# Sample steps of a hybrid decoder: cached rows turned on VectorE, scores in 32x32 tiles, copies on ScalarE

## What is computed

```python
def mla_sample(q_nope, q_rope, ckv_new, kr_new, cache_lat, cache_kr, page_table, w_uk, w_uv):
    lat_past = cache_lat[page_table].reshape(Bd, -1, MLA_KV_RANK)      # 8 x 4096 x 128
    kr_past = cache_kr[page_table].reshape(Bd, -1, MLA_ROPE)           # 8 x 4096 x 32
    q_lat = jnp.einsum('bshn,rhn->bshr', q_nope, w_uk)
    s_past = jnp.einsum('bshr,btr->bhst', q_lat, lat_past) + jnp.einsum('bshp,btp->bhst', q_rope, kr_past)
    ...
    p = jax.nn.softmax(s, axis=-1).astype(lat_all.dtype)
    o_lat = jnp.einsum('bhst,btr->bshr', p, lat_all)
    return jnp.einsum('bshr,rhv->bshv', o_lat, w_uv)
```

## Time and profile before

| | us |
|---|---|
| median of 3 runs (745.23 to 751.47) | 745.68 |
| profiled execution, device time | 743.97 |
| its span, first to last instruction | 742.1 |
| mean granted TensorE clock | 0.995 of full speed |
| TensorE busy | 705.5 (95%) |
| VectorE busy | 355.3 (48%) |
| ScalarE busy | 327.3 (44%) |
| GpSimd busy | 75.6 (10%) |
| HBM read, written | 62.26 MB, 6.07 MB |

### The profile page before, as it was taken

One profiled execution on the slowest core, in us unless ns is written; L12 is line 12 of the kernel. 1 busy time (PEld: TensorE's weight loads), 2 busy tenths in 40 slices (PEclk: granted clock), 3 DMA queues, 4 the chain that ended last, 5 costly groups with the idle time before them and its releaser, 6 DMA issues.

```text
span 742.1 us, 16684 instructions
## 1 busy us (share of the span) xinstructions
PE 705.5 (95%) x7025; PEld 546.4 (74%) x7025; DVE 355.3 (48%) x782; ACT 327.3 (44%) x779; POOL 75.6 (10%) x113
## 2 busy tenths in 40 slices
PE   2799999999999999999999999999999999999995
PEld 1486878788789986777766666777677889678884
DVE  0454380030202025777675576667671111389977
ACT  1254651121212137667656566645675667602100
POOL 0000000000000010101111201132113443000000
PEclk9999999999999999999999999999999999999999
DMA  9995300303001011000010000202756774103332
GB/s 293 396 375 174 114 0 1 114 0 97 0 1 57 1 43 51 9 14 11 10 11 1 1 1 1 59 1 76 240 183 222 274 267 175 60 1 116 123 132 85
DMA packets 35301, 70.31 MB, mean 95 GB/s; under 512 B 6626, under 2 KB 17979, under 8 KB 33564
## 3 DMA queue, kind: packets, MB, share of 16 engines
q1 hardware_dynamic: 30602, 47.73, 19.8%
q0 software_dynamic: 4016, 20.97, 8.1%
q10 hardware_dynamic: 610, 0.55, 0.3%
HBM read 62.26 MB, written 6.07 MB: 92 GB/s over the span
## 4 chain that ended last, share of the span: by engine, by line
PE 90%; DVE 3%; SPq 2%; DMA 2%; ACT 1%; issue 1%; another core or an unknown queue 1%; DVEq 0%; ACTq 0%
PE banks L1988 21%; PE banks L2174 8%; PE banks L2000 6%; PE banks L2302 5%; PE banks L2383 4%; PE banks L2403 3%; PE banks L2152 3%; PE banks L2512 3%; PE banks L2514 3%; PE banks L2513 2%; PE banks L2090 2%; PE banks L2009 2%; PE banks L2452 2%; PE banks L2471 2%; PE banks L2495 2%; DMA s_x<-in_x_prompt 2%
## 5 line engine op out<-in xcount | busy, mean ns | idle before, releaser
L1044 ACT ACTIVATE s_z<-banks 128x512 f32<-128x512 f32 (+3 forms) x40 | 19.6, 501 | 130.0 <-PE banks L1988 130.0
L1988 PE MATMUL banks<-s_w_parts,s_h_b 128*128 128x272 f32 (+3 forms) x328 | 68.0, 323 | 0.0
L1253 ACT ACTIVATE s_z<-banks 128x512 f32<-128x512 f32 (+2 forms) x88 | 41.4, 517 | 47.1 <-PE banks L2383 46.3
L1417 DVE COPY s_zs<-banks 8x512 f32<-8x512 f32 (+3 forms) x6 | 3.5, 576 | 118.5 <-PE banks L1962 118.5
L1988 PEld LDWEIGHTS banks<-s_w_parts,s_h_b 128*128 128x128 f32 x328 | 49.3, 189 | 4.9 <-issue 1.7
L1244 ACT ACTIVATE s_z<-banks,s_temps 128x896 f32<-128x896 f32 (+7 forms) x64 | 47.2, 742 | 11.6 <-DVE s_temps L1712 8.6
L1988 PE MATMUL banks<-s_w_parts,s_h_a 128*128 128x256 f32 (+2 forms) x256 | 49.7, 314 | 0.0
L1988 PE MATMUL banks<-s_z_r,s_h_b 128*128 128x512 f32 (+1 forms) x152 | 48.8, 387 | 0.0
L2383 PEld LDWEIGHTS banks<-s_ident,s_z 128*128 128x128 f32 x288 | 33.3, 141 | 11.8 <-issue 5.5
L2383 PE MATMUL banks<-s_ident,s_z 128*128 128x128 f32 x288 | 39.8, 274 | 1.6 <-DVE s_z L1728 1.6
L1988 PE MATMUL banks<-s_z_r,s_h_a 128*128 128x512 f32 x128 | 40.9, 395 | 0.0
(11 more groups left out here) (391 smaller groups left out, 1520.7 us busy)
## 6 DMA issues: line engine op xcount, KB each, us to landing
s_z<-in_w_ada SPq DMA_DIRECT2D x16, 512.0 KB, 12.2
s_temps<-in_w_in SPq DMA_DIRECT2D x3, 2048.0 KB, 7.7
s_x<-in_x_prompt SPq DMA_DIRECT2D x8, 512.0 KB, 11.8
s_z<-in_w_ada SPq DMA_DIRECT2D x1, 4096.0 KB, 13.8
s_kt<-in_w_out SPq DMA_DIRECT2D x8, 512.0 KB
s_temps<-in_x_prompt SPq DMA_DIRECT2D x8, 512.0 KB
out_y_prompt<-s_temps SPq DMA_DIRECT2D x7, 512.0 KB
s_temps<-in_w_in SPq DMA_DIRECT2D x2, 832.0 KB, 14.2
```

Of the source, the lines that this page charges most:

```text
L1253: nc.scalar.activation(PTb[r % 3][:, 4 * g:4 * g + n, :], banks[:, 4 + (groups(r) + g) % 2, 0:P * n].rearrange("p (j q) -> p j q", j=n), A ...
L1988: last = nc.tensor.matmul(banks[:, proj_bank(c, t), 0:WIDTH[c]], h_[half][:, k, n0:n0 + P], w_, start=(k == 0 and n == 0), stop=(k == KT - ...
```

## The change

Nothing outside the sample steps is computed differently. In words:

- TensorE no longer transposes cached rows. VectorE turns them in SBUF with its own transpose, which turns each 32x32 block in place: two instructions of 128x1024 (`keys_turned`) and one of 128x512 (`rotary_turned`) for each step. Those of step n + 1 come before and after the maximum of step n. Unit 0 is turned at the end of the prompt's score steps.
- Because only blocks are turned, the contraction is split into four groups of 32 partitions that hold different tokens, and into k = 0 to 3 for the four quarters of the 128 numbers, and k = 4 for the rotary part. The scores are 5 x 4 x 4 = 80 matmuls of 32x32 weights with 128 columns; row group g writes to bank g, column group c to partitions 32c on. The result is 128 partitions by 4 x 128 columns; on each 32 partitions only the first eight, the heads, mean something.
- The queries are stored as 32x32 pieces (`q_tiles`), filled by 16 small copies on VectorE from `q_lat`.
- The maximum goes over 512 columns in four banks and the exponential over 512 columns; the weights are turned by four transposes instead of one.
- The copies of turned weights and of weighted sums move from VectorE to ScalarE; ScalarE's five copies of turned rows are gone.
- `p_s` has one buffer instead of two, and the scores four banks with one buffer.
- The gate products move from the end to steps 3, 5, 7 and 9, into banks 4 and 5; the copies of w_out are placed differently among ScalarE's last steps.
- In the merge, one more VectorE instruction (`nm_own`) masks the meaningless partitions.

The diff, cut to its core:

```diff
-        qlw = carve(NB * 56, NB, 56)
-        qrw = carve(NB * 32, NB, 32)
+        q_lat = carve(NB * H)
+        q_tiles = carve(NB * 5 * H + 24)
+        nm_own = carve(NB * SPLITS, NB, SPLITS)
         o_new = carve(NB * (KVR + 1), NB, KVR + 1, rows=H)
...
+        def latT(n, half):
+
+            return slab(FIRST_KEYS[half]) if n % 2 == 0 else latT1[:, SEQ * half:SEQ * half + SEQ]
+
...
+        def tile_queries(b, k):
+
+            c0 = H * (5 * b + k)
...
+        GATES_AT = (3, 5, 7, 9)
...
+            def weights(n):
+
+                act.wait_ge(f_mx, n + 1)
+                if n >= 1:
+                    act.wait_ge(f_pT, n)
+                b, c = divmod(n, HALVES)
+                nc.scalar.activation(p_s.rearrange("p (r g y) -> p g r y", r=4, g=4), banks[:, 0:4, 0:P].rearrange("p g (r y) -> p g r y", r=4),
+                                     ACT.Exp, bias=nm[:, b, c:c + 1], accum_out=o_all[:, b, c, KVR:KVR + 1]).then_inc(f_p, 1)
...
+            def weights_out(n):
+                act.wait_ge(f_pT, n + 1)
                 if n >= 2:
-                    act.wait_ge(f_sc, n - 1)
...
+                    act.wait_ge(f_o, n - 1)
+                nc.scalar.activation(pTx[n % 2].rearrange("p (g r) q -> p r g q", g=4)[:, :, :, 0:H],
+                                     banks[:, 6, :].rearrange("p (r g q) -> p r g q", r=4, g=4)[:, :, :, 0:H], ACT.Copy).then_inc(f_pTc, 1)
...
+            def values_out(n):
...
+                act.wait_ge(f_o, n + 1)
+                nc.scalar.activation(o_all[:, b, c, 0:KVR], banks[:, 7, 0:KVR], ACT.Copy).then_inc(f_oc, 1)
...
-            keys_out(0, 4)
             act.wait_ge(mixed, N_PAIRS_OF_HEADS)
-            for j in range(5):
-                keys_out(1, j)
-            weights(0)
+            act.wait_ge(p_padded, 7)
             for n in range(NSTEPS):
-                if n + 2 < NSTEPS:
-                    for j in range(5):
-                        keys_out(n + 2, j)
-                if n + 1 < NSTEPS:
-                    weights(n + 1)
-                if n == NSTEPS - 4:
+                weights(n)
+                if n > 0:
+                    values_out(n - 1)
+                weights_out(n)
+                for q in range(2):
+                    if n == GATES_AT[q] + 1:
+                        act.wait_ge(gate_b, q + 1)
+                        nc.scalar.activation(gateP[:, 512 * q:512 * q + 512], banks[:, 4 + q, :], ACT.Copy).then_inc(gate_bc, 1)
+                    if n == GATES_AT[2 + q] + 1:
+                        act.wait_ge(gate_b, q + 3)
+                        nc.scalar.activation(gateS[:, 512 * q:512 * q + 512], banks[0:NB, 4 + q, :], ACT.Copy).then_inc(gate_bc, 1)
...
                     high_mixed(0)
...
                     act.wait_ge(f_o, 13)
-                    act.wait_ge(f_sc, 15)
-                    for k in range(4):
+                    for k in range(2):
                         high_out(k)
                 if n == NSTEPS - 2:
+                    act.wait_ge(f_sc, 15)
+                    for k in range(2, 4):
+                        high_out(k)
+                if n == NSTEPS - 1:
                     act.wait_ge(f_o, 14)
                     high_out(4)
                     high_out(5)
                     act.wait_ge(f_o, 15)
                     high_out(6)
+                    values_out(n)
                     high_out(7)
...
-            act.wait_ge(gate_b, 2)
-            for q in range(2):
-                nc.scalar.activation(gateP[:, 512 * q:512 * q + 512], banks[:, q, :], ACT.Copy).then_inc(gate_bc, 1)
-                nc.scalar.activation(gateS[:, 512 * q:512 * q + 512], banks[0:NB, 2 + q, :], ACT.Copy).then_inc(gate_bc, 1)
...
+                    nc.vector.tensor_copy(q_tiles[:, 0:NB * 5 * H].rearrange("p (b k h) -> p b k h", b=NB, k=5)[:, :, 4, :],
+                                          banks[:, 7, 64:128].rearrange("p (h b) -> p b h", h=H)).then_inc(p_free, 1)
                 if n == PREP["qlat"]:
                     dve.wait_ge(p_pe, n)
-                    nc.vector.tensor_copy(qlw[:, :, 24:24 + H], banks[:, 7, 0:64].rearrange("p (h b) -> p b h", h=H)).then_inc(p_free, 1)
+                    nc.vector.tensor_copy(q_lat.rearrange("p (b h) -> p b h", b=NB),
+                                          banks[:, 7, 0:64].rearrange("p (h b) -> p b h", h=H)).then_inc(p_free, 1)
...
+                if PREP["qlat"] <= n < PREP["qlat"] + 4:
+                    k = n - PREP["qlat"]
+                    dve.wait_ge(p_free, PREP["qlat"])
+                    for g in range(4):
+                        nc.vector.tensor_copy(q_tiles[32 * g:32 * g + 32, 0:NB * 5 * H].rearrange("p (b k h) -> p b k h", b=NB, k=5)[:, :, k, :],
+                                              q_lat[32 * k:32 * k + 32, :].rearrange("p (b h) -> p b h", b=NB)).then_inc(p_tiles, 1)
...
+            def keys_turned(n, half):
+
+                dve.wait_ge(f_in[n % UNITS], (48 if n % UNITS == 2 else 32) * (n // UNITS + 1))
+                if n >= 2:
+                    dve.wait_ge(f_sc, n - 1)
+                nc.vector.transpose(latT(n, half), rows_of(n, half)).then_inc(f_T, 1)
+
+            def rotary_turned(n):
+                if n >= 2:
+                    dve.wait_ge(f_sc, n - 1)
+                nc.vector.transpose(kroT[n % 2], kro[n % UNITS]).then_inc(f_T, 1)
...
+                if s == len(STEPS):
+                    dve.wait_ge(pt_done, groups(len(STEPS) - LAG))
+                    keys_turned(0, 0)
+                if s == len(STEPS) + 1:
+                    dve.wait_ge(pv_done, N_PAIRS_OF_HEADS - 1)
+                    rotary_turned(0)
+                    keys_turned(0, 1)
...
-                nc.vector.tensor_reduce(nm[:, b, c:c + 1], banks[:, 5, 0:P], AX_X, ALU.max, negate=True).then_inc(f_mx, 1)
-
-            def weights_out(n):
-                dve.wait_ge(f_pT, n + 1)
-                if n >= 2:
-                    dve.wait_ge(f_o, n - 1)
-                nc.vector.tensor_copy(pTx[n % 2][:, :, :, 0:H],
-                                      banks[:, 6, 0:P].rearrange("p (g r q) -> p g r q", g=4, r=4)).then_inc(f_pTc, 1)
-
-            def values_out(n):
-                b, c = divmod(n, HALVES)
-                dve.wait_ge(f_o, n + 1)
-                nc.vector.tensor_copy(o_all[:, b, c, 0:KVR], banks[:, 7, 0:KVR]).then_inc(f_oc, 1)
+                nc.vector.tensor_reduce(nm[:, b, c:c + 1], banks[:, 0:4, 0:P], AX_XY, ALU.max, negate=True).then_inc(f_mx, 1)
...
             dve.wait_ge(mixed, N_PAIRS_OF_HEADS)
-            largest(0)
-            dve.wait_ge(p_padded, 7)
             for n in range(NSTEPS):
-                weights_out(n)
                 if n + 1 < NSTEPS:
-                    largest(n + 1)
-                if n + 1 == NSTEPS:
-                    dve.wait_ge(f_mx, NSTEPS)
-                    nc.vector.tensor_reduce(nmin, nm, AX_X, ALU.min).then_inc(f_dm, 1)
-                values_out(n)
+                    keys_turned(n + 1, 0)
+                    rotary_turned(n + 1)
+                largest(n)
+                if n + 1 < NSTEPS:
+                    keys_turned(n + 1, 1)
+            dve.wait_ge(f_mx, NSTEPS)
+            nc.vector.tensor_scalar(nm_own, nm, floor, None, ALU.max).then_inc(chain_d, 1)
...
-            def keys_transposed(n, j):
...
             def scores(n):
-                pe.wait_ge(f_Tc, 5 * n + 5)
+                pe.wait_ge(f_T, 3 * n + 3)
                 if n >= 1:
                     pe.wait_ge(f_p, n)
-                for r in range(4):
-                    for g in range(4):
-                        nc.tensor.matmul(banks[32 * g:32 * g + 32, 5, 0:P], qlw[:, n // HALVES, 24 - H * r:56 - H * r],
-                                         latT(n, g)[:, P * r:P * r + P], start=(r == 0), stop=False)
-                for g in range(4):
-                    last = nc.tensor.matmul(banks[32 * g:32 * g + 32, 5, 0:P], qrw[:, n // HALVES, :], kroT[n % 2][:, g, :], start=False, stop=True)
+                for k in range(5):
+                    for c in range(4):
+                        for g in range(4):
+                            rows = slice(32 * g, 32 * g + 32)
+                            if k < 4:
+                                keys = latT(n, c // 2).rearrange("p (r k y) -> p r k y", r=SUBS, k=4)[rows, 4 * (c % 2):4 * (c % 2) + 4, k, :]
+                            else:
+                                keys = kroT[n % 2][rows, P * c:P * c + P]
+                            last = nc.tensor.matmul(banks[32 * c:32 * c + 32, g, 0:P], tile_queries(n // HALVES, k)[rows, :], keys,
+                                                    start=(k == 0), stop=(k == 4))
                 last.then_inc(f_sc, 1)
 
             def weights_transposed(n):
                 pe.wait_ge(f_p, n + 1)
                 if n >= 1:
                     pe.wait_ge(f_pTc, n)
-                nc.tensor.transpose(banks[:, 6, 0:P], p_s[n % 2], ident[:]).then_inc(f_pT, 1)
```

(45 more changed lines are left out.)

88 lines of the change are left out of this document (30 added, 58 removed).

## The result

The changed kernel takes 792.44 us (792.03 to 796.03), against 746.3 us for the kernel before in the same comparison: a ratio of 1.062, 95% interval 1.058 to 1.065. It is slower, as forecast, but by 46 us instead of 16, and it lies above the forecast range (747 to 781). The profiled execution has a span of 790.1 us, 48.0 more than before.

A forecast was written before the change was run, and what follows sets the result against it. TensorE's instruction supply was taken to bound the kernel. 557.6 + 23 x 3.9 + 2.3 + 1.6 = 651.2 against 634.72, 16.5 us later; 743.97 + 16.5 = 760.5, 1.7 below the median, so 762 (range 747 to 781).

The forecast's parts named there:

- the 3.9 us a packet: Sample steps: time per TensorE instruction packet with gathers running, chosen between 3.2 and 5.9; 1.54 packets make a 6.0 us step.
- Start: Before the steps: last weighted products start near 555.7, not 557.66; first packet asked for near 557.6, starting 0.8 us later.
- beside a busy TensorE: Before the steps: 13 additional small copies filling q_tiles were taken as covered; without cover they cost up to 3.8 us.
- 23 packets: From last products to step 15's scores: 6,269 TensorE instructions, 384 already there, the other 5,885 fetched at 3.9 us a packet.
- Last packet: End of step 15: 2.3 us for the last packet's work plus 1.6 for maximum and exponential.
- 3.2 without load: Lower bound of a packet's turnaround, request to usable, read at three TensorE stops with DMA nearly idle: 3.2 us.
- with about three ahead: Steps with gathers: an instruction packet waits behind about three gather packets of 0.24 us each, giving 3.9 us a packet.
- The upper bound of the turnaround: Time per instruction packet while gathers run: at most 5.9 us, from the old steps, which it did not hold up.
- (a): Sample steps: instruction supply keeps up, the engine sum holds with steps near 3.9 us; 732 us, chance 0.15.
- (b): Sample steps: instruction supply without contention, 3.3 us a packet; 748 us, chance 0.12.
- (c): Sample steps: array or VectorE slower than nearest rows; slow scores give 6.6 us steps, 774 us; chance 0.08 with (d).
- (d): Sample steps: VectorE transposes and POOL's descriptor writes shut each other out, 6.2 us, near 765; chance 0.08 with (c).

The follow-up runs named there:

- run 3: The kernel before with 52 small matmuls more behind each step's scores, as many instructions as the changed kernel: 794.7 us, ratio 1.070.
- run 7: The changed kernel with the 16 query copies on ScalarE and 32 columns of weights again in the products with the new key: 788.9 us, ratio 1.062.
- run 4: The changed kernel without the eleven gathers of steps 5 to 15: 770.4 us (766.1 and 774.8).
- run 6: The kernel before without the gathers of steps 5 to 15: 743.3 us, ratio 0.995.
- Run 1: The changed kernel with the score matmuls of k = 1, 2, 3 over 32 columns instead of 128, as many instructions: 794.8 us.
- 8: Against the changed kernel: 128x32 query tables, 20 score matmuls, weights turned by 16 matmuls, query copies on ScalarE, 211 instructions a step: 742.8 us, ratio 1.000.
- 9: The version with 128x32 query tables (211 instructions a step) without the gathers of steps 5 to 15: 729.2 us, ratio 0.978.

## Why the prediction was wrong

**Direction and mechanism: right.** TensorE's instruction supply decides. 69 packets, idle time inside the scores' own loop ended by "issue", VectorE waiting for scores: all three signs that the prediction named are there (a packet per 4.8 us is a little above its 3.3 to 4.5), and run 3 brings the slowness into a kernel without any other part of the change.

**The size: wrong in the 3.9 us a packet above all, and in the start.** The exponential of step 15 ends at 682.63 instead of the forecast 651.2, 31.4 us later. Along the forecast's own sum:

- *Start.* The first packet was to begin at 557.6 + 0.8 = 558.4; it began at 564.41, 6.0 later. The last weighted products start at 561.47 and not at 555.7. The gain of the removed transposes is there (the lag behind the kernel before falls from 5.45 us at 502 us to 3.81, so 1.64 of the 2 forecast). But 3.25 us were lost between 485 and 508, on two edits that the prediction costed at nothing: the small copies, "beside a busy TensorE", stood ahead of the normalising of weights that TensorE waited for (run 7), and the products with the new key grew from 1.10 to 1.97 us. The prediction had the copies' price without cover, up to 3.8; TensorE waited 2.0 us behind them. Another 2.2 us of lag was there before 485 us, where nothing is changed: 0.9 in the first 30 us and 1.1 at 297, where the granted clock dropped to 1.2 GHz for a moment in this execution and not in the other.
- *23 packets.* They take 5.04 us each instead of 3.9: 26.2 us. The first takes 9.95, with GpSimd's four DMA instructions of gathers 3 and 4 beside it and the exposed chain of step 0 (TensorE waits 1.8 us for the first exponential). The other 22 take 4.82: 0.86 above the 3.96 that run 4 has without gathers.
- *Last packet.* 2.3 us from the start of the 24th to the end of the exponential instead of 3.1.

6.0 + 26.2 - 0.8 = 31.4. Inside the 26.2, the 3.9 us were made of two terms, 3.2 without load and 0.7 for the gathers, and both failed.

The first is "at 3.2 us a packet the step can't be under 5.0 us", taken as what a packet will take. 3.2 is a least distance, read where TensorE had nothing else to wait for, and the least in the steps was even 3.4 to 3.5. Without gathers 3.96 were measured, in distances from 3.44 to 4.94: 0.76 more for each of 22 packets, 16.7 us. My reading of it, not tested by a run of its own, is that the prediction took the larger of two limits, supply and the chain through maximum, exponential and transposes, where they add up in part. A packet whose instructions fall into a wait of the chain takes longer, and the next one doesn't make up for it; TensorE waits 5.9 us in all for exponentials over these packets.

The second is "with about three ahead", three records of 0.24 us. In the step shown a fetch waited 2.3 to 2.5 us for the rest of a gather's share. A gather starts right behind the weighted sums, each step, and of the eighteen packets up to the end of the last gather at 662 us eleven began inside one. That the mean came out near the forecast, 0.86 us a packet instead of 0.7, or 3.5 us in all, is luck: few long waits and the descriptors' part instead of a short wait for each. The rest of the 26.2 is the first packet, 6.05 us over. How the 16.7 and the 3.5 share is uncertain by the 8.7 us between the two executions of run 4; their sum isn't.

The kernel before could have warned: one of its packet distances in the steps is 9.00 us and its range was 4.6 to 9.0, but with no time lost except the two steps of 5.76 us. These two were left unexplained; run 6 shows that they were the gathers' price already.

**Bounds.** The upper bound of the turnaround, 5.9, would have given 23 x 5.9, or 46 us above the forecast; the range stopped at 781 because contention was given one value and not its own two ends. That is where the range was too narrow.

**The rivals.** (a) *The engines' sum* is refuted in its supply half, and its size was also off. Its terms as they stand there, 2 us and 14 x 0.69 less 1 and less a half, make 10 us and not 13 to 14, so the rival's time would have been 735 and not 732. The last step of the changed kernel has no gather and no late packet, and takes 4.50 us (676.61 to 681.11) instead of 3.86:

```profile
677.34 0.69 ACT L1279 ACTIVATE s_z<-banks,s_temps 128x512 f32<-128x512 f32 x1 [1.95 <-DVE s_temps L1793]
678.17 0.66 PE L2472 MATMUL banks<-s_ident,s_z 128*128 128x128 f32 x4 [0.58 <-ACT s_z L1279]
678.75 2.32 PE L2463 MATMUL banks<-s_z,s_temps 32*32 32x128 f32 x160
681.11 0.69 DVE L1793 TENSOR_REDUCE s_temps<-banks 128x1 f32<-128x512 f32 x1 [2.66 <-PE banks L2463]
```

The scores take 2.32 us where 1.70 was priced from L2090: 0.013 us a pair of records instead of 0.009. So even with instructions at hand the new step would be no shorter than the old 4.55. (b) *Supply without contention* was to give 748; without gathers the time is 770, because 3.96 us and not 3.3 is what a packet takes on average in the traced execution (766 in the other). 3.4 to 3.5 us is the least that occurs. (c) Neither slow tiles nor slow transposes: the block transposes took what the prediction chose, 1.22 and 0.67 us.

```profile
L1754 DVE STREAM_TRANSPOSE s_z<-s_z 128x1024 f32<-128x1024 f32 x18 | 21.5, 1218 | 0.0
...
L1759 DVE STREAM_TRANSPOSE s_z<-s_temps 128x512 f32<-128x512 f32 x7 | 4.7, 673 | 0.0
```

(d) *VectorE and GpSimd shutting each other out:* the longest of the 32 large transposes took 1.245 us, also beside GpSimd's DMA instructions, and those took 0.94 us as before. Not seen.

**The clock.** It fell to 0.88 on average over the 22 packets, as TensorE stood idle. It isn't the cause: it was at full speed in the long stop shown above, and without gathers, at 0.93, a packet still took 3.96 us. Run 1 had it lower still (0.59 to 0.84 in its steps' windows of 20 us) and took 2.4 us longer, which is no clear difference.

## What to carry to other kernels

Count instructions beside time. Where TensorE issues more than about one fetch packet (256 instructions) in 4 us, its instruction stream and not the array set the pace here, and small tiles raise the count without raising the cost of anything that a timeline shows. A least distance is not a mean: where two limits meet in one loop, supply and a chain of waits, expect more than the larger of them. A price read in a quiet stretch holds only for a quiet stretch: look up which transfers run in the stretch where it will be used, and take the length of their whole burst as the other bound. Before multiplying a mean transfer time, look at how many transfers stand in a row on one DMA engine. When work leaves an engine, look for who gets instructions, data or buffers through the same DMA engines.

## What the runs showed of the hardware

- An instruction packet of queue q8 holds 256 instructions and is usable 2.2 to 2.7 us after it began to move, in quiet and loaded stretches alike: nearly all of TensorE's stops of over 1 us for "issue" in the steps end there. The shortest distance between two packets was 3.36 to 3.5 us in the changed kernel, its versions with as many instructions, and runs 3, 8 and 9; with gathers of 1.25 MB running it went up to 7.7 us behind the first.
- A whole packet can run off in 1.62 us (32x32 tiles over 128 columns), so supply can be half as fast as the array. The Trainium skill (Runtime: NRT & Kernel Launch, Instruction fetch mechanics) has the fetch of 16 KB blocks as mostly hidden, because dispatch is slower than the refill. In the kernel before that nearly holds (three short stops in the gated linear attention, two steps 1.2 us longer); in the changed one TensorE idles 30.7 us ahead of the scores' loads.
- While GpSimd issues indirect DMAs, TensorE in such code gets a dozen recorded instructions per 0.72 us. Open is which path the two share.
- The products with the new key, two records each, start 0.12 to 0.15 us apart where they alternate between 128 and 32 partitions of contraction, and 0.065 where all have one shape.
- VectorE's transpose of 32x32 blocks in fp32 took 1.22 us for 128x1024, as the fp32 TENSOR_TENSOR of that size in the earlier trace rows, and 0.67 for 128x512.
